# Gate and up weights of a mixture-of-experts kernel split into high and low float32r parts, with eight shared 1 MB weight buffers

## The reference

```python
mod = c_act @ w_ada[l] + b_ada[l]                       # six rows of 1024 per layer
h = rmsnorm(x, norm_ffn_g[l]) * (1 + sc_f) + sh_f
g_sel = argmax(h @ w_gr + b_gr)                         # 1 of 4 groups
top_v, top_i = top_k(e_logits[g_sel], 2)                # 2 of its 8 experts
# 32 experts, rows of each expert padded to blocks of 128
a = xblk @ w_gate[e]                                    # 128x1024 @ 1024x512
b = xblk @ w_up[e]                                      # 128x1024 @ 1024x512
y = (silu(a) * b) @ w_down[e]                           # 128x512 @ 512x1024
x = x + g_f * sum_of_gated_expert_rows(y)
```

## Time and profile before

| what | value |
|---|---|
| runs | 2032.07, 2035.98, 2038.56 us (median 2035.98) |
| span of the profiled execution | 2037.1 us |
| PE busy | 1822.8 us (89%) |
| DVE busy | 1161.0 us (57%) |
| ACT busy | 709.1 us (35%) |
| POOL busy | 249.4 us (12%) |
| DMA | 545.84 MB, mean 268 GB/s |
| first gate matmul of layer 0, last matmul of layer 0's experts | about 504 us, about 1170 us |

### The profile page before, as it was taken

How to read it: one execution, slowest core, us unless ns; L and a number is a source line. 1 busy time by engine, 2 the same in 40 slices (tenths; PEclk the granted TensorE clock), 3 DMA queues, 4 the chain that set the end, 5 groups by cost and what they waited for, 6 DMA issues and landing times. The chain is left out here.

```text
span 2037.1 us, 19183 instructions
## 1 busy us (share of the span) xinstructions
PE 1822.8 (89%) x6845; PEld 1179.1 (58%) x6845; DVE 1161.0 (57%) x1123; ACT 709.1 (35%) x1092; POOL 249.4 (12%) x230
## 2 busy tenths in 40 slices
PE   3898998983999999999999959399999999999990
PEld 3686876872465656565555548345555555555550
DVE  5877675215556565656565665445555656565666
ACT  6221212450343333333333338133333343434332
POOL 1421214202001010101000000000000000000000
PEclk9898998985999999999999979599999999999995
DMA  9699422117589899999999782139899989899966
GB/s 307 235 307 300 160 83 83 42 64 276 181 321 334 321 341 326 340 330 329 339 323 348 282 312 107 52 135 341 321 339 324 343 324 337 324 337 327 338 226 259
DMA packets 236580, 545.84 MB, mean 268 GB/s; under 512 B 20915, under 2 KB 39911, under 8 KB 236533
## 3 DMA queue, kind: packets, MB, share of 16 engines
q1 hardware_dynamic: 203310, 496.93, 68.1%
q0 software_dynamic: 18432, 33.60, 4.4%
q10 hardware_dynamic: 14792, 14.70, 2.1%
HBM read 532.56 MB, written 46.15 MB: 284 GB/s over the span
## 5 line engine op out<-in xcount | busy, mean ns | idle before, releaser
L1581 PE MATMUL ps<-gate_w,block_columns 128*128 128x512 f32 x1024 | 456.7, 600 | 10.7 <-ACT block_columns L861 10.7
L1584 PE MATMUL ps<-up_w,block_columns 128*128 128x512 f32 x1024 | 449.9, 593 | 0.0
L861 ACT ACTIVATE block_columns<-ps,mod_columns,a_ffn 128x128 f32<-128x128 f32 x512 | 185.5, 467 | 507.0 <-PE ps L1436 507.0
L1289 DVE TENSOR_TENSOR down_w_low<-down_w,down_w_high 128x4096 fp32r<-128x4096 f32 x62 | 274.4, 4426 | 124.2 <-ACT down_w_high L921 124.2
L1584 PEld LDWEIGHTS ps<-up_w,block_columns 128*128 128x128 f32 x1024 | 195.1, 190 | 244.4 <-issue 244.4
L1581 PEld LDWEIGHTS ps<-gate_w,block_columns 128*128 128x128 f32 x1024 | 192.3, 193 | 229.7 <-issue 217.7
L921 ACT ACTIVATE down_w_high<-down_w 128x4096 fp32r<-128x4096 f32 x62 | 224.3, 3618 | 159.8 <-PE ps L1600 159.8
L1279 DVE RECIPROCAL sigmoid_tmp<-sigmoid_tmp 128x512 f32<-128x512 f32 x64 | 214.6, 3353 | 2.2
L1310 DVE COPY scatter_index<-assignment 128x1 uint32 (+1 forms) x64 | 9.8, 153 | 356.8 <-PE ps L1600 356.8
L1598 PE MATMUL ps<-down_w_high,act_columns_high 128*128 128x512 f32 x496 | 200.4, 404 | 0.0
L1599 PE MATMUL ps<-down_w_low,act_columns_high 128*128 128x512 f32 x512 | 199.8, 390 | 0.0
(11 more groups left out here) (238 smaller groups left out, 2050.3 us busy)
## 6 DMA issues: line engine op xcount, KB each, us to landing
gate_w<-in_moe_w_gate_dram SPq DMA_DIRECT2D x64, 2048.0 KB, 15.3
up_w<-in_moe_w_up_dram SPq DMA_DIRECT2D x64, 2048.0 KB, 20.3
down_w<-in_moe_w_down_dram SPq DMA_DIRECT2D x64, 2048.0 KB, 8.2
cond_w<-in_w_ada_dram SPq DMA_DIRECT2D x80, 512.0 KB, 5.5
y_in<-expert_rows SPq DMA_DIRECT2D x16, 1024.0 KB, 7.3
x_rows<-in_x_dram SPq DMA_DIRECT2D x8, 1024.0 KB, 7.9
cond_w<-in_w_ada_dram SPq DMA_DIRECT2D x8, 1024.0 KB, 11.0
in_w<-in_w_in_even_dram ACTq DMA_DIRECT2D x12, 512.0 KB, 7.7
```

The lines of the kernel that those rows point to most:

```text
L861: last = a.activation(dst[:, k, :], src[:, k * P:(k + 1) * P], ACT.Identity, scale=a_f[l][:, k:k + 1], bias=mod[l][:, SH_F, k:k + 1])
L1289: return v.tensor_tensor(down_lo[s][:, :, :], down_w[s][:, :, :], high[:, :, :].bitcast(F32), ALU.subtract)
L1581: lg = mm(BANK[0], xT[s][:, q, :], gate_w[s][:, q, :], start=q == 0, stop=q == KD - 1)
L1584: lu = mm(BANK[1], xT[s][:, q, :], up_w[s][:, q, :], start=q == 0, stop=q == KD - 1)
```

## The change

All three weight matrices of an expert are split now. An expert becomes six units of 1 MB (`G0 G1 U0 U1 D0 D1`); a partition reads one run of 8 KB for each. Eight buffers `raw` are shared by all units in the order in which PE uses them. ACT writes the high part of a unit to one of six fixed `high` tiles, DVE writes the low part over the raw data, and PE does 12 float32r matmuls per gate or up unit and 12 per down unit. The load of unit i waits for the end of PE's work on unit i-8. The silu is one ACT instruction, and DVE multiplies it with the up result in one instruction, which also reorders the columns. The rows are modulated once per tile on DVE, before they are stored, so the block's transposes are copied by one ACT instruction (high) and one DVE subtraction (low). All loops are unrolled, with index and gate columns read in place. Eight modulation rows are stored to DRAM, four of them through a DVE instruction that folds a gain in.

```diff
+        UNIT = 2 * D
+        raw = [at(f"unit{s}", [P, UNIT], W0 + 8 * KB * s) for s in range(SLOTS)]
+        low = [at(f"unit_low{s}", [P, UNIT], W0 + 8 * KB * s, F32R) for s in range(SLOTS)]
+        high = [at(f"unit_high{k}", [P, UNIT], SE + 8 * KB * k, F32R) for k in range(len(KINDS))]
...
+            def load_unit(i):
+                if i >= SLOTS:
+                    sp.wait_ge(unit_done, i - SLOTS + 1)
+                n, kind = UNITS_OF[i]
+                l, e, h = n // NE, n % NE, int(kind[1])
+                if kind[0] == "D":
+                    src = moe_w_down[l, e].rearrange("(p h k) d -> h p (k d)", p=P, h=2)
+                else:
+                    src = (moe_w_gate if kind[0] == "G" else moe_w_up)[l, e].rearrange("(p h k) f -> h p (k f)", p=P, h=2)
+                sp.dma_start(raw[i % SLOTS][:, :], src[h]).then_inc(unit_loaded[i % SLOTS], 16)
...
+            def part_high(n, kind):
+                i, k = AT[n, kind], KINDS.index(kind)
+                act.wait_ge(unit_loaded[i % SLOTS], 16 * (i // SLOTS + 1))
+                if n:
+                    act.wait_ge(unit_done, AT[n - 1, kind] + 1)
+                act.wait_ge(unit_high, i) if i else None
+                a.activation(high[k][:, :], raw[i % SLOTS][:, :], ACT.Copy).then_inc(unit_high, 1)
...
+                for n in range(n0, n0 + NE):            # ACT
+                    if n > n0:
+                        act_high(n - 1)
+                        part_high(n - 1, "D0")
+                        part_high(n - 1, "D1")
+                    silu(n)
+                    if n + 1 < n0 + NE:
+                        part_high(n + 1, "G0")
+                        part_high(n + 1, "G1")
+                        part_high(n + 1, "U0")
+                        block_columns(n + 1)
+                        part_high(n + 1, "U1")
...
+                for n in range(n0, n0 + NE):            # DVE
+                    if n >= n0 + 2:
+                        results(n - 2)
+                    if n > n0:
+                        low_part_of_act(n - 1)
+                        part_low(n - 1, "D0")
+                        part_low(n - 1, "D1")
+                    if n + 1 < n0 + NE:
+                        part_low(n + 1, "G0")
+                    activation_rows(n)
+                    if n + 1 < n0 + NE:
+                        low_part_of_rows(n + 1)
+                        part_low(n + 1, "G1")
+                        part_low(n + 1, "U0")
+                        part_low(n + 1, "U1")
...
+            def gate_unit(n, kind):
+                i, k = AT[n, kind], KINDS.index(kind)
+                dst, h = BANK[0 if kind[0] == "G" else 1], int(kind[1])
+                pe.wait_ge(unit_low, i + 1)
+                for j in range(KD // 2):
+                    q, cols = h * (KD // 2) + j, slice(j * FE, (j + 1) * FE)
+                    mm(dst, xT_hi[:, q, :], high[k][:, cols], start=q == 0, stop=False)
+                    mm(dst, xT_hi[:, q, :], low[i % SLOTS][:, cols], start=False, stop=False)
+                    last = mm(dst, xT_lo[:, q, :], high[k][:, cols], start=False, stop=q == KD - 1)
+                last.then_inc(unit_done, 1)
...
+            def entry_rows(l, t):                       # DVE, replaces the row copy on ACT
+                ch.link(v.reciprocal(rstd[:, which, t:t + 1], sd[:, which, t:t + 1]))
+                ch.link(v.scalar_tensor_tensor(out=tmp_row[l][:, :], in0=xr[:, t, :], scalar=rstd[:, which, t:t + 1],
+                                               in1=a_ffn[l][:, :], op0=ALU.mult, op1=ALU.mult))
+                v.tensor_tensor(xn[t % 2][:, :].rearrange("p (k q) -> p q k", q=P),
+                                tmp_row[l][:, :].rearrange("p (q k) -> p q k", k=KD),
+                                b_ffn[l][:, :].rearrange("p (q k) -> p q k", k=KD), ALU.add).then_inc(xn_ready, 1)
...
+            def gained_row(n):
+                dve.wait_ge(gain_loaded, 16 * (i + 1))
+                dve.wait_ge(row_stored, 16 * STORED.index(n))
+                v.scalar_tensor_tensor(out=row_kept[0:1, :], in0=ROWS[n % 2][0:1, :], scalar=GAIN_OF[PARTS[n]][1],
+                                       in1=gain_in[0:1, :], op0=ALU.add, op1=ALU.mult).then_inc(row_out, 1)
```

More of the change, by code:

```diff
@@ L80, in hybrid_trunk @@
     SH_M, SC_M, G_M, SH_F, SC_F, G_F = range(NMOD)
-    HEAD, TAIL = 3, 3
-    PAIRS = (NE - HEAD - TAIL) // 2
-    PAIR = (HEAD, HEAD + 1)
+    KINDS = ("G0", "G1", "U0", "U1", "D0", "D1")
+    UNITS_OF = []
+    for l in range(LAYERS):
+        for e in range(NE + 1):
+            n = l * NE + e
+            UNITS_OF += [(n, kind) for kind in KINDS[:4]] if e < NE else []
+            UNITS_OF += [(n - 1, kind) for kind in KINDS[4:]] if e else []
+    AT = {unit: i for i, unit in enumerate(UNITS_OF)}
+    SLOTS = 8
     xv = x[0].rearrange("(t p) d -> p t d", p=P)
@@ L471, in _ @@
             sp.wait_ge(acc_init, 2)
[L472 to L476, removed]
+            for n in range(len(PARTS)):
+                part_loads(n)
             sp.wait_ge(part_summed, len(PARTS))
@@ L818, in _ @@
                 n = PART_BEHIND.get(u)
[L819 to L830 removed]
+                if n is not None:
+                    part_row(n)
                 if u == 8 * KA - 4:
@@ L936, in act_block, with block_columns, silu, act_high @@
+            def block_columns(n):
+                act.wait_ge(b_T, n + 1)
+                if n % NE:
+                    act.wait_ge(unit_done, AT[n - 1, "U1"] + 1)
+                columns(xT_hi, PT).then_inc(xT_high, 1)
+            def silu(n):
+                act.wait_ge(unit_done, AT[n, "G1"] + 1)
+                if n:
+                    act.wait_ge(act_ready, n)
+                a.activation(sig[:, :], BANK[0], ACT.Silu).then_inc(silu_ready, 1)
+            def act_high(n):
                 act.wait_ge(act_T, n + 1)
-                act_high().then_inc(aT_hi_ready, 1)
+                if n:
+                    act.wait_ge(unit_done, AT[n - 1, "D1"] + 1)
+                a.activation(aT_hi[:, :, :], PM.rearrange("p (k q) -> p k q", q=P), ACT.Copy).then_inc(aT_hi_ready, 1)
@@ L1268, in further_blocks @@
                 v.sem_inc(extra_ready, 1)
-            def gather_index(e, loaded, s):
-                if loaded is not None:
-                    dve.wait_ge(xg_loaded[s], loaded)
-                v.tensor_copy(idx_g[s][:, :], tok[:, ds(e, 1)]).then_inc(idx_g_ready, 1)
-            def silu_mul(done, chain):
-                chain.link(v.tensor_scalar(sig[:, :], sig[:, :], 1.0, None, ALU.add))
-                chain.link(v.reciprocal(sig[:, :], sig[:, :]))
-                chain.link(v.tensor_tensor(act_r[:, :], BANK[0], sig[:, :], ALU.mult))
-                done()
@@ L1361, in moe @@
+                last = n0 + NE - 1
+                results(last - 1)
+                low_part_of_act(last)
+                part_low(last, "D0")
+                part_low(last, "D1")
+                results(last)
                 m = more[l]
```

658 lines of the change are left out of this document (287 added, 371 removed).

## The result

The changed kernel takes 1866.55 us (median of 4 runs, 1863.87 to 1869.1), the one before 2037.2 us in the same runs: ratio 0.917, 95% interval 0.9157 to 0.9182. The forecast was 1883.0. The profiled execution has a span of 1865.7 us, 171.4 less than before.

The account below looks back on a forecast made before the run. PE bounds the expert loop at 20.54 us a block, DMA close behind; PE 17.9, DVE 17.7, DMA 17.2 plus 0.2 give 18.1. 64 blocks save 156 us, the rest adds 3: 1884 span, 1883 us median, range 1858 to 1960.

Parts of the forecast that it names:

- DVE 17.7: Expert block on DVE: six subtractions 13.3 to 13.75 us plus smaller operations; upper end 18.1, taken as 17.7 us.
- DMA 17.2: Expert block's 6.83 MB of loads: bounds 16.6 us (412 GB/s, full queue) to 18.8 us (by share), taken as 17.2.
- About 15 us held: Weight buffers: slot held about 15 us of a 23.9 us turn, leaving 9 us for a 1 MB load.
- DVE's waits: Expert block: DVE running 1.4 to 4.8 us behind PE's U1 never waits, nor does PE wait for it.
- The rest: Everything outside the 64 blocks: ends 5.8, starts -1, entry of rows -6, modulation +4, together +3 us.
- Ends: Ends of the two expert stages: 9.7 us of work in place of 6.8, +2.9 each, +5.8 us.
- rival 4: PE idles enough at each unit for the clock to fall to 1.2 GHz; chance 0.08 together with rival 2.
- Modulation: Four gained rows of 1.28 us on DVE, four sums more on PE: +4 us, if not hidden +10.
- Entry of rows: Mixer stages' row tiles: -12 for last tiles, +6 in layer 1's mixer; together -6 us, from -12 to +12.
- Rival 1: DMA binds the expert block at its share's price, 18.8 + 0.1 us a block, 1935 us; chance 0.19.
- Rival 2: Load, ACT, DVE, PE chain closes, DVE's waits stand bare: 21.2 us a block, 2082 us; chance 0.08 with rival 4.
- Rival 3: Late loads or DVE's full 18.1 with waits of 0.8 to 1.2: 19.2 us a block, 1954 us; chance 0.18.

Follow-up runs that it names:

- the second experiment: Changed kernel without the third matmul of each gate and up product, DVE subtracting only the first half of each unit's columns: 1843.48 us, 0.9062.
- the version that splits ahead: Changed kernel with the last expert's down units split ahead into high tiles of the gate: 1854.91 us, 0.9109.
- the half-load experiment: Changed kernel without the third gate and up matmul, half of each load, DVE subtracting over as many elements as before: 1822.3 us, 0.8958.
- The all-passes experiment with half the low parts: Changed kernel with all three passes, half of DVE's subtractions, and half loads after the first eight units: 1863.16 us, 0.9158.

## Why the prediction was right, and where its sizes were off

**The block: right in mechanism, 0.4 us too long.** "The three engines stand at 17.9, 17.7 and 17.2" and 0.2 for not meeting gave 18.1; it is 17.74 in layer 0 and 17.69 in layer 1. That term alone is 32 x 0.36 + 32 x 0.41 = 25 us; the rest, 6 us larger than forecast, offsets part of it, and 18 are left between the forecast for the profiled execution (1884) and its span (1865.7). About half of the 0.36 to 0.41 is PE's own price, and the other half is the 0.2, which no run shows. Each part, as measured:

- PE 17.9: with both rivals relieved it is 17.69 and 17.73. I took the gate at the down's 5.57, step between precisions included. Gate and up together are 725.13 - 714.11 = 11.02, so 5.51 each, and the activation transposes are 0.35 for 0.44.
- DVE 17.7: its floor is 17.04, 0.66 less. I took the upper end of the subtraction, 2.29, six times (13.75). The back-to-back distance of 2.20 makes 13.2; half of 4426 ns, the lower end, was the right one. The product's stride did cost what its bound said, 0.69 to 1.09.
- DMA 17.2: no run measured its floor bare. With PE relieved of a pass it moved 392 GB/s at share 1.00 from 600 to 1000 us, and the block of 6.83 MB (385 GB/s over the same stretch x 17.74 us) needs 17.4 us at that; DVE was full there too, so the DMA's own floor may be lower. The value between the bounds held; 412 GB/s was the peak of a microsecond, not a rate that lasts. The Trainium skill ("DMA: Bandwidth & Descriptors", Bandwidth) has about 358 GB/s for each core when both cores of a domain stream and 425 for one alone. Only one core runs here, so it is the second that applies, and 385 to 396 GB/s lie below it. The prediction set the first against a measured 412, but no run here has two cores streaming.
- The 0.2 for not meeting: it is nothing that can be seen. With DVE and the DMA relieved, and with both of them full, a layer's block is 17.69 or 17.73 to 17.74, and PE has no wait from 600 to 1000 us.

I had placed the DMA as the lowest of the three; it is the second, 0.3 below PE by the 17.4, and DVE is the lowest.

**"Fewer and longer runs should cost no more per byte": right, and worth a price I had not given them.** They move the DMA from just above PE to just below it, which is 17.3 us of the whole time.

**"About 15 us held, it holds, with little to spare": half right.** The ring holds, and the 15 us is measured at 14.9. But it is no fixed price: 2 of them are ACT's lead, which it gives up when slots are short, so seven slots hold too. The prediction also set the 9 us that are free against 8.3 for a load of 2 MB. That was the down tile's; in the same view of the earlier trace rows the other two of the same size land much later:

```profile
gate_w<-in_moe_w_gate_dram SPq DMA_DIRECT2D x10, 2048.0 KB, 15.3
up_w<-in_moe_w_up_dram SPq DMA_DIRECT2D x10, 2048.0 KB, 20.3
```

In the changed kernel a load of 1 MB lands 7.9 us after its issue on average, while one lands every 2.95 us. So about three loads are on their way at a time, and I read most of the 7.9 as the turn of the others.

**DVE's waits: right.** From 600 to 1000 us DVE never waits for the up result, and for the rows 11.7 us in all, 0.5 a block and at most 1.7; PE loses nothing by it. The second experiment shows the other side of the band: a DVE that is ahead waits, and PE pays.

**The rest: +9 for +3, and that it came so near is luck.** Three of its terms were off by 4 to 10 us, in both directions. Ends, +5.8 for both: a layer's end costs 12.24 - 6.92 = 5.3 in layer 0, and 11.20 - 6.89 = 4.3 in layer 1, together 9.6. The missing part is the clock. PE stood for 4.90 us until the first low part was there, and restarted slowly (length of the stretch, PE, PEld, DVE, ACT, POOL, clock, share, GB/s):

```profile
1072.00:1076.00 4.00, 3.00 (x7) 2.45 (x8) 3.06 (x2) 0.55 (x1) 0.00 (x0) 0.50 0.47 190
1076.00:1081.00 5.00, 5.00 (x18) 3.72 (x17) 0.00 (x0) 0.00 (x0) 0.00 (x0) 0.79 0.02 3
```

A granted clock of 0.50 is the lower level, 1.2 GHz. The first twelve matmuls start 0.43 us apart and the next ones 0.23, so the clock costs about 2.4 us of this end. It is the mechanism of rival 4, at a stage's end. In the version that splits ahead PE idles 1.54 there, the clock stays at 1.00 until the last matmul, and the 24 matmuls take 5.8 us instead of 8.1. Modulation, forecast +4: the stretch up to layer 0's first residual became 5.1 shorter instead (349.82 to 344.71), in part by a PE stall on DVE's sums that fell:

```profile
189.71 2.94 PE L1451 MATMUL ps<-cond_acc,ones 128*128 128x512 f32 x4 [2.98 <-DVEq L1068]
```

where before the stall at the same place was 5.28. That ACT waits for DVE's gained row (39.0 us in three waits, 11.2 in another) did not make that stretch longer: right. Entry of rows, forecast -6: from the first residual to the logits layer 0 became 0.4 longer, and from the combine to the logits layer 1's mixer 3.2. I had the strided write at up to 0.7 a tile. It costs that in layer 1, where its median is 1949 ns against 1225 for a plain operation of that size; the group of the eight in layer 0 has a mean of 2595, so 1.4 a tile:

```profile
L1136 DVE TENSOR_TENSOR xn<-modulate_tmp,ffn_shift_row 128x1024 f32<-128x1024 f32 x8 | 20.8, 2595 | 0.3
```

**The rivals.** Rival 1 fell: 1.00 of the share carried 387 GB/s, so share was no price per byte. Its mechanism is real at short runs, and even there the price is 18.1, not 18.9. Rival 2 did not decide, since DVE idles 0.5 us a block and not 2.8; six slots and the half low parts show its two halves. Rival 3 is not seen. Rival 4 is seen at the stage's end. In the loop of the changed kernel the granted clock is 1.00, but not in experiments in which PE waits longer: it is 0.93 in the second experiment, 0.98 with six slots and 0.95 with the silu on DVE.

## What to carry to other kernels

Take an operation's price in a queue from start to start, not from its duration: on DVE, six times 0.09 us (2.29 for 2.20) were most of the 0.66 between my 17.7 and the measured 17.04. When three engines come out within a few per cent, ask what each alone would take and test that, because what a part of the change is worth depends on which is on top: the silu's move was worth nothing before and 233 us after, the 8 KB runs 17 us. A landing time in a full queue, and the time for which a buffer is held, both hold slack; how many buffers are needed is told by taking one away. A stage's end, where the pipeline drains, is the place to look next: there an idle PE pays twice, for the wait and for the clock.

## What the runs showed of the hardware

**GpSimd's indirect DMA instructions take longer beside a busier DVE.** The same instruction takes the time below on POOL, from 600 to 1000 us (groups; count, busy us, mean ns). Before, with DVE at 56%:

```profile
L701 POOL DMA_INDIRECT gathered<-normed_rows,gather_index x19 | 19.4, 1020 | 113.3 <-DVE gather_index L1274 113.3
L707 POOL DMA_INDIRECT expert_rows<-y_out,scatter_index x19 | 19.0, 1002 | 238.5 <-DVE y_out L1312 238.5
```

after, with DVE at 97%:

```profile
L704 POOL DMA_INDIRECT expert_rows<-y_out,assignment x22 | 67.3, 3059 | 274.9 <-DVE y_out L1308 274.9
L698 POOL DMA_INDIRECT gathered<-normed_rows,token x23 | 43.1, 1872 | 7.1 <-issue 7.1
```

and in the half-load experiment, with DVE at 100% and the DMA share at 0.69:

```profile
L704 POOL DMA_INDIRECT expert_rows<-y_out,assignment x24 | 174.3, 7262 | 202.9 <-DVE y_out L1309 202.9
```

The all-passes experiment with half the low parts (DVE 62%, share 0.67) shows 1.41 for the gather and 1.01 for the scatter. The second experiment has the same 62% of DVE at a share of 0.97, and there they are 1.57 and 1.79. So the load of the DMA is not needed to make them long, as the 7.26 at 0.69 shows, but it may take part. An unbroken row of DVE operations goes with the longest ones, though not always: the gather of the half-load experiment shows 1.02. It stayed hidden here, since scatter and gather have most of a block. Why it happens no run tells apart.

**Relieving DVE made the kernel slower** by 8 us (second experiment). The blocks became uneven, and PE's waits for the rows' low part rose from 13.4 to 57.0 us of the 400, with the granted clock at 0.93 instead of 1.00.
